# Two transformer blocks on one core: attention heads taken in pairs, the first weight tile loaded in halves, and five reorderings of small vector work

## Chip, cores and metric

One Trainium2 chip, of which the kernel uses one core. The metric is the device time of one execution in microseconds (us); several executions give a median. The engines are TensorE (PE, matrix products and transposes by the identity), VectorE (DVE), ScalarE (ACT), GpSimd (POOL) and SyncE (SP, which here only issues the loads of weights).

## The reference, cut to what matters

Two blocks run one after the other on x of 256 rows by 1024 columns, float32.

```python
for i in range(2):                        # first block
    h = h + (neighbourhood_attention, short_conv_mixer)[i](rms_norm(h))
    h = h + peer_mixer(rms_norm(h))       # top 16 of 2 x 128 keys, 8 heads, 16384 experts
h = rms_norm(h)
# second block
mem_n = rms_norm(mem)
# even layer: heads of 64: 8 over selected blocks (nsa_s), 8 over a window (nsa_w), 8 moba, 4 over mem (mem_e)
#   plus 8 heads over 15 compressed blocks; y = cat(a_out * silu(nz), b_out * silu(mz), m_out * silu(ez)) @ w_out
# odd layer: 4 retention heads, 4 heads over mem (mem_o)
out = rms_norm(odd_layer(even_layer(h)))
```

peer_mixer scores each row against 128 + 128 keys for each of 8 heads, takes the top 16 of each side, the top 16 of their sums, and a weighted sum of `gelu(x @ w_up[e])  * w_down[e]` over the chosen experts. The kernel computes it densely: products with all 16384 rows of w_up, a weight for each (zero where not chosen), and a product with all of w_down.

## The kernel before, in words

All products are done at full float32 precision by splitting each operand into a high part (rounded) and a low part (the rest): high x high, low x high and high x low. A **unit** is a tile of 512 KB of weights, 128 partitions by 1024 numbers, and there are some 730 of them in one fixed order, loaded by SP into a ring of buffers `raw`. ACT copies each into `wh` (line 1458, `highs(end)`: all units up to `end` and a fixed number ahead), DVE subtracts to make `wl` (line 1895, `lows(end)`), and PE multiplies by both. PE takes a unit's high part first, calls `middle`, then takes the low part, then calls `after`. In the order written out by hand, each engine's program says between which units it does its other work.

**Start.** x comes in four parts of 256 KB (`load_x`), the first two of them ahead of the first unit. DVE scales x by the gains, ACT rounds it (`attn_high`), DVE makes the low part (`attn_low`). ACT squares x for the row scales, POOL makes the scales from them, and PE turns them (`turn_rows`).

**Turnovers.** When wo, conv_out, even_out or odd_out ends, DVE adds the product to the residual by quarters (`add_quarters`, line 2012 for wo; line 2010 for conv_out), PE transposes the new residual (`turn`, line 914), DVE scales it (line 1933), ACT rounds it and DVE makes its low part (line 1941), and then the next product starts. wo is taken in the order `WO_ORDER`, which finishes columns 0 to 511 two units ahead of the rest; conv_out takes all four units of one half and then all four of the other.

**peer_mixer.** The query product is followed by the scores; then PE takes the up phase, in which a unit lasts one **tile** of about 2.8 us. Meanwhile DVE finds the top 16 and makes the choices (`pstep`, lines 2143 to 2231). Between its steps it does the low parts: `between(ns)` adds the priced time of a step to a counter and makes a low when the counter has reached `LOW_EVERY`. The prices are written by hand. During the down phase (gated tiles, line 1107) ACT makes `gh` (line 1659) and DVE `gl` (line 2277) for each tile of about 2.7 us. In the second down phase the norm of `mem` is done too: four squares at tile 80 (`norm`), the scales and, at tile 98, `norm_parts` and `norm_split` for all four groups at once.

**Even layer.** 36 units of even_in. PLAN tables say after which unit which step comes: rotation of projections (`rope`, lines 2516 to 2520), transposes, the compressed branch (`vc`, `hid`, `kvc`, `cmp_S`, ...), and from unit 15 on the 28 **heads**. Each head has three steps: S (scores by PE, line 1023; DVE scales and masks them, line 2024, and takes the maximum, line 2038; ACT takes exponents, line 1532), T (PE transposes the weights, line 1028; ACT copies them out of the bank, line 1445) and O (product with v, line 1035; DVE multiplies by the reciprocal of the sum, lines 2654 to 2670). T comes one unit after S and O two units after. There are eight banks in PSUM; four (`other`) go round for all these steps in the order of the jobs, so that a job waits until the job four before it has been read out.

```python
EV_S = (15, 16, 17, 18, 19, 20, 20, 21, 21, 22, 22, 23, 23, 24, 24, 25,
        25, 26, 26, 27, 27, 28, 29, 29, 30, 30, 31, 31)
EV = [(kind, a) for n in range(37) for kind, lag in (("S", 0), ("T", 1), ("O", 2)) ...]
```

## Time and profile before

| what | value |
|---|---|
| median of 3 runs | 2330.66 us (2330.3 to 2331.43) |
| the profiled execution: its own time | 2331.18 us |
| the profiled execution: span in the trace | 2329.4 us |
| mean granted clock of TensorE | 0.999 |
| PE busy | 2302.6 us, 99% of the span |
| DVE, ACT, POOL busy | 1693.9, 1389.1, 128.7 us |
| loaded from memory | 394.5 MB, 170 GB/s over the span |

The profile shows one execution. Busy time is that of an engine's own instructions. A row of a wait names the instruction that waited and the one that released it; L12 is line 12 of the kernel. Names in rows: `bank` is a PSUM bank, `wh`, `wl` the high and low parts of a unit, `x_both` both parts of the normalized input, `arena` and `aux` the working memory, `small` a tile of scalars per row.

### The profile page before, as it was taken

To read this page: it belongs to the slowest core of one execution; us is meant where nothing else is said; L and a number is where in the kernel's file an instruction comes from. 1 tells how busy PE (TensorE), PEld (TensorE's weight loads), DVE (VectorE), ACT (ScalarE), POOL (GpSimd) and SP (SyncE) were. 2 spreads that over 40 slices of the span, in tenths; PEclk is the share of its full clock that TensorE was granted. 3 is DMA by queue.
4 is the path that set the end of the run, shared out by engine and by line. 5 is a ranking of instruction groups with operands and counts; after the bars stand their busy time and mean duration, and the time that the engine had idled before them with its cause. 6 is when DMAs were issued, how large, how long until landed. Compare 5 with 4: busy or idle time off the path is not lost.

```text
span 2329.4 us, 43671 instructions
## 1 busy us (share of the span) xinstructions
PE 2302.6 (99%) x14764; PEld 2032.4 (87%) x14764; DVE 1693.9 (73%) x3202; ACT 1389.1 (60%) x2562; POOL 128.7 (6%) x196
## 2 busy tenths in 40 slices
PE   9999999999999999999999999999999999999998
PEld 8889989999888888999899999988888887788877
DVE  6767996899755555775998799956656668867565
ACT  5646666887545455445666787755554555765554
POOL 1001121000000000000211100000000000000000
PEclk9999999999999999999999999999999999999999
DMA  7455555444566666556555544466665654246454
GB/s 241 134 170 160 186 182 181 144 140 143 177 194 191 194 191 194 177 180 191 172 181 182 167 142 144 148 205 191 193 205 177 197 175 127 82 131 196 136 160 146
DMA packets 137460, 397.58 MB, mean 171 GB/s; under 512 B 12465, under 2 KB 13793, under 8 KB 136545
## 3 DMA queue, kind: packets, MB, share of 16 engines
q1 hardware_dynamic: 134432, 384.71, 53.4%
q0 software_dynamic: 2448, 10.56, 1.3%
q8 instruction: 90, 1.47, 0.3%
q14 instruction: 58, 0.47, 0.1%
q10 hardware_dynamic: 432, 0.36, 0.0%
HBM read 394.54 MB, written 1.05 MB: 170 GB/s over the span
## 4 chain that ended last, share of the span: by engine, by line
PE 86%; DVE 9%; issue 3%; ACT 2%; DVEq 0%; POOL 0%; ACTq 0%; POOLq 0%
PE bank L1107 29%; PE bank L1091 16%; PE bank L976 11%; PE bank L1079 8%; PE bank L982 7%; PE bank L1083 4%; PE bank L1120 4%; DVE wl L1895 2%; PE bank L1035 1%; ACT wh L1458 1%; PE bank L1183 1%; PE bank L1023 1%; PE bank L1028 1%; PE bank L1008 1%; PE bank L1059 1%
## 5 line engine op out<-in xcount | busy, mean ns | idle before, releaser
L1895 DVE TENSOR_TENSOR wl<-raw,wh 128x1024 fp32r<-128x1024 f32 x726 | 886.2, 1222 | 499.9 <-ACT wh L1458 488.1
L1458 ACT ACTIVATE wh<-raw 128x1024 fp32r<-128x1024 f32 x726 | 765.0, 1054 | 616.2 <-PE bank L1107 326.5
L1091 PE MATMUL bank<-x_both,wh 128*128 128x256 f32 x2304 | 303.9, 285 | 0.0
L1091 PEld LDWEIGHTS bank<-x_both,wh 128*128 128x128 f32 x2304 | 285.8, 191 | 0.0
L1107 PE MATMUL bank<-wh,gl 128*128 128x512 f32 x992 | 265.8, 390 | 1.7 <-DVE gl L2277 1.7
L1107 PE MATMUL bank<-wh,gh 128*128 128x512 f32 x992 | 265.5, 389 | 0.5 <-ACT gh L1659 0.5
L1107 PE MATMUL bank<-wl,gh 128*128 128x512 f32 x992 | 265.2, 389 | 0.0
L1079 PE MATMUL bank<-x_both,wh 128*128 128x512 f32 x896 | 224.9, 393 | 0.0
L1107 PEld LDWEIGHTS bank<-wh,gl 128*128 128x128 f32 x992 | 185.8, 188 | 41.9 <-DVE gl L2277 3.5
L1107 PEld LDWEIGHTS bank<-wh,gh 128*128 128x128 f32 x992 | 185.9, 188 | 39.5 <-ACT gh L1659 1.1
L1107 PEld LDWEIGHTS bank<-wl,gh 128*128 128x128 f32 x992 | 186.2, 188 | 38.7
L976 PE MATMUL bank<-wh,x_both 128*128 128x512 f32 (+1 forms) x768 | 195.9, 397 | 1.0 <-ACT wh L1458 0.8
L1079 PEld LDWEIGHTS bank<-x_both,wh 128*128 128x128 f32 x896 | 161.1, 189 | 28.8
L976 PEld LDWEIGHTS bank<-wh,x_both 128*128 128x128 f32 x768 | 139.5, 189 | 31.3 <-issue 4.6
L1091 PE MATMUL bank<-x_both,wl 128*128 128x256 f32 x1152 | 162.9, 284 | 2.3 <-DVE wl L1895 2.3
L1640 ACT ACTIVATE first<-onehot,weight_high 128x128 bf16<-128x128 bf16 x512 | 160.7, 396 | 2.1 <-PE bank L1120 1.8
L1091 PEld LDWEIGHTS bank<-x_both,wl 128*128 128x128 f32 x1152 | 148.3, 192 | 4.5 <-DVE wl L1895 3.9
L1083 PEld LDWEIGHTS bank<-x_both,wl 128*128 128x128 f32 x896 | 122.1, 190 | 9.3 <-DVE wl L1895 0.7
L1575 ACT ACTIVATE halves<-bank 128x512 f32<-128x512 f32 x112 | 67.0, 598 | 101.0 <-PE bank L1083 101.0
L1083 PE MATMUL bank<-x_both,wl 128*128 128x256 f32 x896 | 125.1, 282 | 0.0
L2252 DVE TENSOR_TENSOR first<-onehot,rest_pairs 128x512 bf16<-128x512 bf16 x256 | 99.4, 429 | 26.4 <-PE bank L1120 22.7
L822 POOL TENSOR_TENSOR arena<-halves 128x256 f32 (+1 forms) x112 | 85.7, 765 | 360.1 <-ACT halves L1575 360.1
(327 smaller groups left out, 2883.6 us busy)
## 6 DMA issues: line engine op xcount, KB each, us to landing
raw<-in_w_upT SPq DMA_DIRECT2D x256, 512.0 KB, 3.5
raw<-in_w_down SPq DMA_DIRECT2D x256, 512.0 KB, 4.2
raw<-in_l_w_in SPq DMA_DIRECT2D x84, 512.0 KB, 3.7
raw<-in_peer_w_query SPq DMA_DIRECT2D x32, 512.0 KB, 3.8
raw<-in_l_w_out SPq DMA_DIRECT2D x28, 512.0 KB, 3.3
raw<-in_attn_w_qkv SPq DMA_DIRECT2D x24, 512.0 KB, 4.2
raw<-in_conv_w_in SPq DMA_DIRECT2D x24, 512.0 KB, 3.9
arena<-in_na_bias POOLq DMA_DIRECT2D x4, 1024.0 KB, 6.4
```

The costliest lines, as they stand in the source:

```text
L822: pool.tensor_tensor(acts[:, bass.ds(i * 4 + t, 1), :].rearrange("p a b -> p (a b)"), halves[:, 0], halves[:, 1], ALU.add)\
L976: last = pe.matmul(bank(js[b])[:, 0:cols], lhsT=x[:, kt, b * P:(b + 1) * P], rhs=w[part][:, kk, :], **flags)
L982: last = pe.matmul(bank(js[b])[:, m * SEQ:(m + 1) * SEQ], lhsT=w[part][:, kk, c0:c0 + P], rhs=x[:, kt, :], **f)
L1079: pe.matmul(banks[b].rearrange("p (a b) -> p a b", a=2), lhsT=w[0][:, k, :], rhs=x_both[:, :, k, :], start=k == 0, stop=False, skip_group_ ...
L1083: last = pe.matmul(banks[b][:, 0:SEQ], lhsT=w[1][:, k, :], rhs=xh[:, k, :], start=False, stop=k == KT - 1, skip_group_check=True)
L1091: last = pe.matmul(banks[b][:, 0:SEQ], lhsT=w[part][:, k, :], rhs=x_in[xp][:, k, :], start=(k == 0 and part == 0 and xp == 0), stop=(k == ...
L1107: last = pe.matmul(banks[4 + 2 * m + h][:, :], lhsT=g[gp][:, m * P:(m + 1) * P], rhs=w[:, h * 512:(h + 1) * 512], start=start and part == ...
L1120: last = pe.matmul(banks[2 + q % OUTS][:, c * N_KEYS:(c + 1) * N_KEYS], lhsT=onehot[:, q % RING, c, 1, :], rhs=first[:, q % FIRSTS, p, c, ...
L1458: act.activation(unit_parts(n)[0][:, 0:kts * cols], raw[:, n % RAW, 0:kts * cols], ACT.Copy)\
L1640: ins = act.activation(first[:, q % FIRSTS, 0, c, :], onehot[:, q % RING, c, 0, :], ACT.Copy, scale=weight_high[:, c0:c0 + 1])
L1895: tt(lo[:, 0:kts * cols], raw[:, n % RAW, 0:kts * cols], hi[:, 0:kts * cols].bitcast(F32), ALU.subtract)\
L2252: last = tt(first[:, q % FIRSTS, 1 + p].rearrange("p c (n b) -> p c n b", b=2), onehot[:, s, :, 0].rearrange("p c (n b) -> p c n b", b=2), ...
```

## The change

1. **Start.** The first unit is loaded in two halves of 256 KB with a semaphore each, and ACT rounds it by halves, between its work on x; ACT's squares of parts 0 and 1 of x come first of all; DVE makes the low part of unit 2 ahead of x's parts 2 and 3; there is one more warm-up product.
2. **Turnovers.** In wo and conv_out, DVE makes one low part, not two, ahead of the first two quarters' adds. conv_out is taken in `WO_ORDER`, and the turn comes after its seventh unit (`CONV_TURN`).
3. **Queries.** ACT takes one more unit's high part ahead of its rounding of the last two groups of the rescaled input.
4. **Choices.** `LOW_EVERY` 1400 in place of 1250; new prices; the product with `key_of` in two halves of four heads; the sums and choices of the second stage one or two tiles later.
5. **Memory norm.** One square per tile (80 to 83), scales six tiles later, and the eight rounding steps spread over tiles 98 to 105 by `MEM_STEPS`.
6. **Even and odd layer.** Heads in pairs: the S of a pair at the end of unit n (`EV_AT`), its T between the high and the low part of unit n + 2, its O in the same place of unit n + 3, with one bank for both O. DVE takes one maximum over both heads for each t, one reciprocal, one gate product, and one product for the four outputs of a pair (two where it adds or multiplies into what is there). Three memsets of DVE go to POOL, ahead of the layer; the four copies of `kvc` into the block diagonal become one product with a mask.

```diff
...
-WO_TURN, OUT_TURN, EVEN_TURN, ROWS_AFTER, ROWS_EARLY, ROWS_CONV = 30, 1, 2, 7, 2, 3
+WO_TURN, CONV_TURN, EVEN_TURN, ROWS_AFTER, ROWS_EARLY, ROWS_CONV = 30, 6, 2, 7, 2, 3
...
-EXP_TILES, SUM_TILES, CHOICE_TILES = (26, 54), (30, 59), (34, 62)
+EXP_TILES, SUM_TILES, CHOICE_TILES = (26, 54), (31, 61), (35, 63)
...
-LOW_EVERY = 1250
+MEM_STEPS = ([("whole", 0)], [("whole", 1), ("high", 0)], [("whole", 2), ("high", 1)], [("low", 0), ("high", 2)],
+             [("whole", 3)], [("low", 1), ("high", 3)], [("low", 2)], [("low", 3)])
+LOW_EVERY = 1400
...
-WARM = (7, 5)
+WARM = (7, 6)
...
-EV_S = (15, 16, 17, 18, 19, 20, 20, 21, 21, 22, 22, 23, 23, 24, 24, 25,
-        25, 26, 26, 27, 27, 28, 29, 29, 30, 30, 31, 31)
-EV = [(kind, a) for n in range(37) for kind, lag in (("S", 0), ("T", 1), ("O", 2)) for a in range(len(EV_S)) if EV_S[a] + lag == n]
...
+EV_AT = (16, 18, 20, 21, 22, 23, 24, 25, 26, 27, 28, 29, 30, 31)
+EV_T, EV_O = 2, 3
...
+                        J.add("evO", len(even_pairs(4 * c + u, EV_O)), ring="other")
+                        J.add("evT", 2 * len(even_pairs(4 * c + u, EV_T)), ring="other")
...
+                            J.add("evS", 2, ring="other")
...
+            for kk, done in enumerate((first_landed, landed[0])):
+                sp.dma_start(raw[:, 0, kk * CHUNK:(kk + 1) * CHUNK], units[0][0][:, kk, :]).then_inc(done, 16)
...
+            pool.memset(cmp_small[:], 0.0)
+            pool.memset(cmp_s, 0.0)
+            pool.memset(block_mask, 0.0).then_inc(mask_cleared, 1)
+            pool.wait_ge(mask_cleared, 1)
+            for i in range(4):
...
+            def pair_outputs(name, p):
+
+                j = take(name + "O", p)
+                for i in range(2):
+                    wait_read(pe, turned_at(name, p, i))
+                    family, _, qT, kT, v = pair_heads[name][2 * p + i]
+                    for t in range(TT):
+                        n = key_tiles(family, t)
+                        for kt in range(n):
+                            last = pe.matmul(bank(j)[:, (i * TT + t) * HEAD:(i * TT + t + 1) * HEAD],
+                                             lhsT=turned_of(name, head_base[name] + 2 * p + i)[:, weight_tiles(family).index((kt, t)), :],
+                                             rhs=v[kt], start=(kt == 0), stop=(kt == n - 1))
+                done(last, j)
...
+            def even_middle(n):
...
-            for c in range(2):
-                project("conv_out", "N", conv_out, k=2 * c, ready=lambda k0: split_ready("conv", k0 // 2 + 1),
-                        after=lambda u: c == 1 and u == OUT_TURN and turn("peer1", "conv", (0, 1)))
+            project_in("conv_out", conv_out, WO_ORDER, lambda i: i == CONV_TURN and turn("peer1", "conv", (0, 1)),
+                       lambda k0: split_ready("conv", k0 // 2 + 1))
...
-            def norm(src, ready, then=None):
-
-                for p in range(4):
-                    ready(p + 1)
-                    c, t = p // 2, p % 2
-                    act.activation(squares[:, p], src[:, t, c * 512:(c + 1) * 512], ACT.Square,
-                                   accum_out=small[:, 2 * t + c:2 * t + c + 1]).then_inc(squared, 1)
-                if then:
...
-                        highs(query + ROWS_AFTER + 2)
-                        highs(query + ROWS_AFTER + 3)
+                        for ahead in (2, 3, 4):
+                            highs(query + ROWS_AFTER + ahead)
                         norm_split(f"rescaled{layer}", some=(2, 3))
...
-                    norm(view(0, TT, D), lambda p: act.wait_ge(extra_loaded["mem"], 16 * TT))
-                    gated_tiles(MEM_SQUARES, MEM_SPLIT)
-                    norm_split("mem", mem_in_T)
-                    gated_tiles(MEM_SPLIT, TAIL[0] - SPLIT)
+                    for p in range(4):
+                        gated_tiles(MEM_SQUARES + p, MEM_SQUARES + p + 1)
+                        mem_squared(p)
+                    gated_tiles(MEM_SQUARES + 4, MEM_SPLIT)
+                    for k, steps in enumerate(MEM_STEPS):
+                        gated_tiles(MEM_SPLIT + k, MEM_SPLIT + k + 1)
...
+            for p in range(2):
+                squared_part(None, p)
             attn_high(0, 0, first_whole, first_high)
+            first_weights_high(0, first_weights)
+            attn_high(1, 0, first_whole, first_high)
+            first_weights_high(1, hi_ready)
+            issued[0] = 1
             attn_high(0, 2, x_whole, x_high)
-            attn_high(1, 0, first_whole, first_high)
-            highs(first_unit["qkv"] - 1)
             attn_high(1, 2, x_whole, x_high)
+            for p in range(2, 4):
+                squared_part(None, p)
...
             norm_split("attn", some=(2, 3))
...
+                        for p in even_pairs(4 * c + u, EV_T):
+                            pair_turned("ev", p)
                         highs(first_unit["even_in"] + KT // UKT * c + u + 1)
                         if u == KT // UKT - 1:
...
-                lows(start, 2)
+                lows(start, 1 if out_name in ("wo", "conv_out") else 2)
                 add_quarters(out_name, (0, 1))
                 lows(turn, 2)
...
-                        pstep(tt(by_head, by_head, key_of[:, :, i].unsqueeze(2).to_broadcast([P, PEER_HEADS, TOPK, TOPK]), ALU.mult), 1200)
-                        for w, ns in ((8, 700), (4, 430), (2, 300)):
+                        for h0 in range(0, PEER_HEADS, PEER_HEADS // 2):
+                            some = by_head[:, h0:h0 + PEER_HEADS // 2]
+                            pstep(tt(some, some, key_of[:, h0:h0 + PEER_HEADS // 2, i].unsqueeze(2)
+                                     .to_broadcast([P, PEER_HEADS // 2, TOPK, TOPK]), ALU.mult), 730)
+                        for w, ns in ((8, 730), (4, 460), (2, 450)):
                             pstep(tt(pick[:, :, 0:w], pick[:, :, 0:w], pick[:, :, w:2 * w], ALU.add), ns)
-                        pstep(tt(top_out(t, i), pick[:, :, 0], pick[:, :, 1], ALU.add))
+                        pstep(tt(top_out(t, i), pick[:, :, 0], pick[:, :, 1], ALU.add), 430)
...
-                    gated_tiles(TRIG + 25, MEM_SQUARES)
+                    gated_tiles(TRIG + 25, MEM_SQUARES + 6)
                     norm_scale("mem")
-                    gated_tiles(MEM_SQUARES, MEM_SPLIT)
...
+                    for k, steps in enumerate(MEM_STEPS):
+                        gated_tiles(MEM_SPLIT + k, MEM_SPLIT + k + 1)
+                        for kind, g in steps:
+                            if kind == "whole":
+                                whole("mem", g)
+                            elif kind == "low":
+                                lower("mem", g, mem_in_T)
...
+            lows(first_unit["qkv"], 2)
             for g in range(2, 4):
                 whole("attn", g)
-            lows(first_unit["qkv"], 2)
...
-                        dve.memset(cmp_small[:], 0.0)
...
-                        for i in range(4):
-                            ins = dve.tensor_copy(vbd[32 * i:32 * i + 32, k, i, :], bank(j)[32 * i:32 * i + 32, 64:64 + HEAD])
-                        read_out(ins, j)
+                        read_out(tt(vbd[:, k], bank(j)[:, 64:64 + HEAD].unsqueeze(1).to_broadcast([P, 4, HEAD]),
+                                    block_mask.unsqueeze(2).to_broadcast([P, 4, HEAD]), ALU.mult), j)
...
-                            step(dve.memset(cmp_s, 0.0))
...
+                top = pair_of(pair_top, p)
+                if family in CAUSAL:
+                    for t in range(TT):
+                        ins = dve.tensor_reduce(top[:, :, t], slots[:, :, t, 0:key_tiles(family, t) * P], AX, ALU.max, negate=True)
+                else:
+                    ins = dve.tensor_reduce(top, slots, AX, ALU.max, negate=True)
+                ins.then_inc(scores_shifted, 2)
...
+                step(dve.reciprocal(pair_scale, pair_sums[:, n % 8:n % 8 + 2]))
...
+                read_out(tt(pair_tmp, out_, by_row, ALU.mult), j)
+                step(tt(dst, dst, pair_tmp, op))
...
-                    even_heads(even_heads_at(4 * c + u, "S"))
+                    for p in even_pairs(4 * c + u, EV_O):
+                        pair_outputs("ev", p)
+                    for p in even_pairs(4 * c + u):
+                        pair_scores("ev", p)
                     if c < len(EVEN_COLS):
                         lows(first_unit["even_in"] + KT // UKT * c + u + 1)
...
```

## Rows read from the trace of the kernel before

**Rows 1.** The page, part 1: busy time and share of the span by engine.
```profile
PE 2302.6 (99%) x14764; PEld 2032.4 (87%) x14764; DVE 1693.9 (73%) x3202; ACT 1389.1 (60%) x2562; POOL 128.7 (6%) x196
```
**Rows 2.** Waits of PE: line <- who released it: total us, times, longest.
```profile
PE bank L982 <- ACT wh L1458: 2.3, 4, 0.9
PE bank L1091 <- DVE wl L1895: 2.3, 4, 0.6
...
PE bank L1107 <- DVE gl L2277: 1.7, 2, 1.4
...
PE bank L914 <- DVE resid L2012: 1.0, 2, 0.7
```
**Rows 3.** Timeline of PE, start: start, length, work [idle before <-releaser].
```profile
8.65 2.15 PE L982 MATMUL bank<-x_both,wh 128*128 128x256 f32 x16 [0.88 <-ACT wh L1458]
...
15.43 1.22 PE L982 MATMUL bank<-x_both,wl 128*128 128x256 f32 x8 [0.87 <-DVE wl L1895]
```
**Rows 4.** DMA issues, first 30 us: count, KB each, median us to landing.
```profile
raw<-in_attn_w_qkv SPq DMA_DIRECT2D x11, 512.0 KB, 4.8
...
resid<-in_x SPq DMA_DIRECT2D x4, 256.0 KB, 4.7
```
**Rows 5.** Timeline of PE and of DVE at the turn in wo.
```profile
138.09 0.71 PE L982 MATMUL bank<-x_raw_h,wh 128*128 128x256 f32 x4 [0.26 <-DVE x_raw_l L1941]
```
```profile
132.72 0.68 DVE L2012 TENSOR_TENSOR resid<-bank,resid 128x512 f32<-128x512 f32 x1
```
**Rows 6.** Timeline of PE in conv_out.
```profile
1031.82 0.70 PE L976 MATMUL bank<-wh,conv_out_h 128*128 128x512 f32 x2 [0.41 <-DVE conv_out_l L2475]
```
**Rows 7.** Timeline of PE in the query product of layer 0.
```profile
175.15 0.71 PE L982 MATMUL bank<-x_raw_h,wh 128*128 128x256 f32 x4 [0.59 <-ACT wh L1458]
```
**Rows 8.** Timeline of DVE in the choices of layer 0.
```profile
265.65 0.88 DVE L2230 TENSOR_TENSOR pick<-pick 128x512 bf16<-128x512 bf16 x2
266.56 0.40 DVE L2231 TENSOR_TENSOR arena<-pick 128x128 f32<-128x128 bf16 x1
266.99 1.23 DVE L2225 TENSOR_TENSOR pick<-places,lanes 128x2048 bf16<-128x2048 bf16 x1
268.25 1.23 DVE L1895 TENSOR_TENSOR wl<-raw,wh 128x1024 fp32r<-128x1024 f32 x1
```
**Rows 9.** Timeline of PE at the second half of the memory norm.
```profile
1789.90 1.20 PE L1107 MATMUL bank<-wh,gh 128*128 128x512 f32 x4 [0.49 <-ACT gh L1659]
```
**Rows 10.** Windows: length, then busy us (instructions) of PE, PEld, DVE, ACT, POOL, granted clock, DMA share, GB/s.
```profile
1905.00:2068.00 163.00, 156.28 (x954) 125.98 (x953) 131.50 (x347) 101.78 (x212) 0.00 (x0) 0.99 0.36 105
```
```profile
1959.00:1963.00 4.00, 4.00 (x17) 3.28 (x15) 3.60 (x9) 1.57 (x5) 0.00 (x0) 0.57 0.46 131
```
**Rows 11.** Timeline of PE among the even layer's heads.
```profile
1958.61 0.52 PE L1028 MATMUL bank<-ident,aux 128*128 128x128 f32 x3 [1.52 <-ACT aux L1532]
1958.89 3.36 PE L976 MATMUL bank<-wh,x_both 128*128 128x512 f32 x8
```
```profile
1976.08 2.11 PE L976 MATMUL bank<-wh,x_both 128*128 128x512 f32 x8
```
**Rows 12.** Groups of DVE, 1905 to 2068 us: count, busy us, mean ns, idle before.
```profile
L2024 DVE SCALAR_TENSOR_TENSOR aux<-bank,aux 128x256 f32<-128x256 f32 x24 | 9.9, 413 | 0.0
L2038 DVE TENSOR_REDUCE small<-aux 128x1 f32<-128x256 f32 x24 | 9.8, 408 | 0.0
...
L2517 DVE TENSOR_TENSOR arena<-arena,aux 128x512 f32<-128x512 f32 x6 | 4.2, 692 | 0.2
...
L2662 DVE TENSOR_SCALAR arena<-bank,small 128x64 f32<-128x64 f32 x16 | 3.8, 280 | 0.3
```
**Rows 13.** Timeline of ACT at the third family's exponents and its silu.
```profile
2051.18 0.51 ACT L1532 ACTIVATE aux<-aux,small 128x256 f32<-128x256 f32 x1
...
2051.80 1.28 ACT L1732 ACT_TABLE_LOAD   x1
2053.09 1.58 ACT L1732 ACTIVATE arena<-arena 128x512 f32<-128x512 f32 x2
```

More of the change, by code:

```diff
@@ L401, in build @@
         weight("conv_in", d["conv_w_in"], 3 * D, CONV_CHUNKS)
-        weight("conv_out", d["conv_w_out"], D)
+        weight_in("conv_out", d["conv_w_out"], WO_ORDER)
         weight("query1", d["peer_w_query"][1], 2048)
@@ L1542, in attention, with pair_exponents, pair_turned @@
                         evac(turned_of(name, n).rearrange("p a b -> p (a b)")[:, 0:w], j, bank(j)[:, 0:w])
+            def pair_exponents(name, p):
+                for i in range(2):
+                    n, family = head_base[name] + 2 * p + i, pair_heads[name][2 * p][0]
+                    act.wait_ge(scores_shifted, n + 1)
+                    for t in range(TT):
+                        row = scores_of(name, n)[:, t, 0:key_tiles(family, t) * P]
+                        ins = act.activation(row, row, ACT.Exp, bias=pair_top[:, n % 4, t:t + 1],
+                                             accum_out=sums_of(name, n)[:, t:t + 1])
+                    ins.then_inc(weights_ready, 1)
+            def pair_turned(name, p):
+                for i in range(2):
+                    w = len(weight_tiles(pair_heads[name][2 * p][0])) * P
+                    j = turned_at(name, p, i)
+                    evac(turned_of(name, head_base[name] + 2 * p + i).rearrange("p a b -> p (a b)")[:, 0:w], j, bank(j)[:, 0:w])
             def peer(layer):
@@ L2295, in gated_tiles @@
                 def gated_tiles(t0, t1):
-                    with dve.Fori(0, (t1 - t0) // 4) as i:
-                        for k in range(t0, t0 + 4):
-                            low(d0 + k, i)
-                            gated_low(k, i)
+                    if t1 - t0 >= 4:
+                        with dve.Fori(0, (t1 - t0) // 4) as i:
+                            for k in range(t0, t0 + 4):
+                                low(d0 + k, i)
+                                gated_low(k, i)
                     for t in range(t1 - (t1 - t0) % 4, t1):
@@ L2476, in _ @@
                             conv_out[0][:, 2 * g:2 * g + 2].bitcast(F32), ALU.subtract), x_low, n)
[L2477 to L2478 removed]
+            start = first_unit["conv_out"] + CONV_TURN
+            turnover("peer1", "conv_out", start, start, first_unit["query1"], x_raw)
             peer(1)
```

239 lines of the change are left out of this document (129 added, 110 removed).

## The prediction

> **What bounds the kernel now.** I read the busy times first. PE is busy for 2302.6 of the 2329.4 us of the span [rows 1], and the change leaves the number of its products alone, but for one more warm-up. So it can win only what PE waits, about 27 us with both ends of the kernel, plus time in which PE is slow. DVE is at 73% and ACT at 60% [rows 1]; their work costs nothing unless PE stands for it. Then I read the waits of PE by releaser [rows 2], and the timeline of PE around each place that the diff touches [rows 3, 6, 7, 9, 11]. The reader is to see many short stalls, none over 1.6 us. They cost more than the bracket shows: successive groups overlap (a group that starts at 1958.61 and lasts 0.52 ends after the next one's start, 1958.89 [rows 11]), and a stall breaks the overlap. So I add 0.15 us to each bracket.
>
> **Start.** PE's first true product waits 0.88 us for ACT's cast of unit 0, the low part of unit 1 waits 0.87 for DVE [rows 3]. With halves, ACT casts 512 columns at a time, and PE begins some 0.5 us earlier, but the low of unit 0 still comes behind both casts. DVE's earlier order takes off most of the second wait, and the squares ahead of ACT's other work take off a later one of some 0.5 us for the row scales. Against it: a 256 KB load took a median 4.7 us to land where 512 KB took 4.8 [rows 4], so a half load is hardly sooner by itself. Value -1.0; bounds 0 (the second half lands as the whole did, and the low part sets the pace) and -1.8 (both waits go).
>
> The Trainium skill (DMA: Bandwidth & Descriptors, Bandwidth) has a rule that speaks against it: batch transfers to 1 MiB or more. Here it agrees with rows 4 in that halves gain little; by it the load's part would be nought and the term about -0.6.
>
> **Turn in wo.** The first add's wait and the second's sum to 1.0 us [rows 2]. The adds take 0.68 [rows 5] and stand behind a low of 1.23 [rows 8] that the change puts after them: both waits go, about 1.3 with restarts. That low and what follows are then later by 1.2 less the stall saved: the wait of the query's first product, 0.26 [rows 5], grows by 0.4 or so. Value -0.8; bounds -0.3 and -1.3.
>
> **Conv_out.** It waits 0.41 us for the low part of the convolution's rows [rows 6], which goes on, since the cast of the next unit is behind ACT's casts of the rows too. In WO_ORDER one unit is left to cover the turn's second half instead of two, a unit being 2.7 us here, while DVE must do two adds of about 0.7 [rows 5], two scalings and two low parts (0.69 each), some 4.1 us. I take +0.8; bounds -0.3 and +1.5.
>
> **Queries.** 0.59 us at 175.15 [rows 7], and its like in layer 1: ACT's cast stands behind its rounding. One cast more ahead takes both off: -1.5 with restarts; bounds -0.8 and -1.5 (its rounding of groups 2 and 3 comes one cast later, which has slack).
>
> **Choices.** Four waits of up to 0.6, 2.3 together [rows 2], and some 0.1 to 0.2 us each for restarts, and again at a second place just behind each: 4.5 in all. The cause is the price list: 0.88 + 0.40 + 1.23 us of steps stand between two lows (265.65 to 268.25) [rows 8], since 430 + 300 + 300 stays below 1250 and the next step is started. With the new prices (460 + 450 + 430, then 1250) that does not fit: no stretch between lows has more than about 1.6 us of steps. A tile is about 2.8 us, a low is 1.23, so 1.6 just fits. Value -3.9; bounds -3.3 and -4.5.
>
> **Memory norm.** DVE's four wholes and lowers stand ahead of a `gl`: 1.7 us in two waits [rows 2], 0.49 for ACT's `gh` [rows 9]; with restarts, and ACT's squares before the first, 3.1. Spread, each tile gets at most two of these steps (0.7 to 0.9 each). In a tile of 2.7 us DVE has 1.23 of low and 0.42 of `gl`, ACT 1.06 and 0.40: 1.0 and 1.2 are left, and the queues have some slack from tile to tile. Value -2.9; bounds -2.3 and -3.1.
>
> **Even layer.** In 1905 to 2068 PE is idle for 163.0 - 156.3 = 6.7 us [rows 10]; with 15 restarts 9.0. On top, after the 1.52 us wait at 1956.7 the granted clock of 1959 to 1963 is 0.57 [rows 10], so mostly the lower of its two levels (1.2 and 2.4 GHz), and eight products take 3.36 us for the usual 2.11 [rows 11]; with six smaller ones, 1.6 lost. So 10.6 is there to win, this with the compressed part's 2.0 at 1914 to 1931.
> What DVE gets back, per pair of masked heads: one reduce of 0.41 for t = 1 becomes one of 0.69 for two (0.82 before), likewise for t = 0, so 0.3; the outputs, four of 0.28 [rows 12], become one of about 0.43, so 0.7; one reciprocal and one gate product go, 0.3. That is 1.3 of about 4.6 us, over 14 pairs about 15 us (less for those that add), and 1.4 of memsets and 0.5 of copies: 17 of DVE's 131.5 us [rows 10]. But the total of DVE is not what makes PE wait; what does is order. I wrote down for each unit when PE, DVE and ACT could start each step, with the durations of such rows; three places come out late:
> (a) T of the first pairs comes one and a half units (about 6 us with the heads' own products) after S. The chain is 0.62 + 0.83 for masking and 0.4 + 0.7 for the maxima on DVE, a cast of 1.06 ahead on ACT, and four exponents of 0.4 to 0.51 with 0.12 after each (2.3): 5.9. It is met or missed by up to 1 us: 1.9 over two pairs.
> (b) Around units 19 to 22 DVE has two rotations, each four steps of 0.4 to 0.69 [rows 12] for two t, 4.5 us, beside lows and pairs of 3.3. It falls some 3.9 behind a unit of 4.6. At the end of unit 22 the transposes of `even_T` 8 need the bank that held the first T of pair 2, and ACT frees it only after the exponents of pair 3, which wait for DVE: 3.0 us, and 1.0 before it.
> (c) The T of the first `mem` pair: ACT has exponents of 2.0 and more, then a table load of 1.28 and silu of 1.58 [rows 13], then a cast, and only then the turned copies that the O in the middle of unit 33 waits for: 1.5.
> The compressed part keeps 1.6 of its 2.0. The memsets stand on POOL ahead of the load of the compression weights, and delay it by some 2 us; POOL does nothing at all from 1905 on [rows 10], and the load is issued long before, so I put that at 0 (if the cover were gone, 2). That makes 9.0 for 9.0 of before, and the clock: the 3.0 wait is twice the one that took it down before. I give that 6 in 10: 0.9 for 1.6. Value -0.7. Bounds: nothing of (a) to (c) comes, -8; or all come in full, and 3.2 of the slow clock, +2.
>
> The Trainium skill (TensorE: Matmul & The Clock Gate, Part 1: The HAM clock gate) says that the array's clock falls by half when idle and comes back after sustained activity. The 0.57 in rows 10 agrees. [...]
>
> **Odd layer.** No wait of PE at its four heads before; the pairs keep its lags of a unit or more: 0, and with its cover gone no more than the 0.5 of one such wait.
>
> **Sum.** -1.0 - 0.8 + 0.8 - 1.5 - 3.9 - 2.9 - 0.7 = -10.0. The profiled execution took 2331.2, so 2321.2 for it; the median is 0.5 lower, so 2320.7. I say 2321.
>
> **Rivals.**
> *New waits in the even layer (0.20).* (b) and (c) come in full, the clock falls twice, and conv_out loses 1.5. For it: four banks for more jobs in a bunch, DVE's 81% of 163 us. Against: five bank jobs per pair where there were six. -10.0 + 2.7 + 0.7 = -6.6; with turnovers at their poor bounds -5: 2325.
> *All goes through (0.18).* DVE's 17 us come out of the stalls directly, (a) to (c) stay below 0.5 each: even layer -7, conv_out 0, the rest as in the sum: -17: 2314. For it: before, the waits of this stretch fall where DVE is busy nearly throughout. Against: (b) is one bunch of work that the pairs do not thin out.
> *The choices gain nothing (0.09).* The real step times drift off the new prices, or the lows are late elsewhere: the sum without -3.9 is -6: 2324.5.
> *Slower (0.05).* DVE falls behind in the up phase. Up to 1.4 of priced steps and then one of up to 1.25 can come between two lows: 1.25 + 1.4 + 1.23 = 3.9 us against a tile of 2.8. It decides if the mean of steps between lows is above 2.8 - 1.23 = 1.6 us. Then each tile costs the excess; 0.2 us over 56 tiles in two layers is +22: 2343. Against: the top-16 steps, 0.28 each, are stopped finely, at 1.4 to 1.6; the mean stays at 1.43 by the old trace's counts.
> My forecast has 0.48.
>
> **Range and chances.** 2316 to 2326: the forecast's own range is 2318 to 2324; the first and third rival lie inside, of the second 0.15 of its 0.18 is below, and the slower one's 0.05 above, which leaves out 0.2. A difference of under 0.2%, 4.7 us, is about what a measurement of this kernel can't tell from none: faster is below 2326.0. From the cases: the forecast 0.47 faster, the first rival 0.14 of its 0.20, all goes through 0.18, the third 0.07 of its 0.09: 0.86. Same: 0.09. Slower: 0.05.
>
> **What would show it.** PE's waits at L914 for DVE's adds at 133 and at L982 for ACT at 174 and 1085 gone; no wait at L1091 for wl over 0.2; no bracket on L1107 near 1736 and 1789; near unit 22 of even_in one wait of 2 to 3 us at the transposes, released by ACT's copy, followed by a clock of about 0.6. I am wrong if the up phase's tiles lengthen (DVE), or if the even layer shows waits under 0.5 only (then it is 2314), or if in conv_out a wait above 1.5 us comes up.

## The result, and the profile after

The changed kernel takes 2315.4 us (median of 4 runs, 2314.09 to 2316.47) against 2330.74 (4 runs, 2330.3 to 2331.43): 0.9933 of before, 95% interval 0.9921 to 0.9946. It is faster by 15.3 us. The forecast was 2321, in 2316 to 2326, so the result lies just below the range. It is beside the rival "all goes through" (2314), though not for that rival's reason. The profiled execution took 2316.47, with a span of 2314.7: 14.7 less than before's.

From page part 1 of the changed kernel, as in [rows 1]:

```profile
PE 2293.9 (99%) x14765; PEld 2029.5 (88%) x14765; DVE 1678.2 (73%) x3109; ACT 1382.6 (60%) x2563; POOL 130.2 (6%) x203
```

PE's busy time is 8.7 us less, with the same products and one more. Part of that belongs to stalls, since the ends of products are modelled and one that stands before a stall counts longer; part, as the next section shows, is PE's own work getting shorter, which the prediction did not look for.

The waits of PE, as in [rows 2]:

```profile
PE bank L1259 <- ACT aux L1500: 2.3, 1, 2.3
PE bank L998 <- DVE x_raw_l L2027: 1.7, 4, 0.5
PE bank L1087 <- ACT aux L1500: 1.5, 1, 1.5
PE bank L1395 <- DVE warm L2449: 1.5, 1, 1.5
PE bank L998 <- DVE x_both L2465: 1.4, 1, 1.4
PE bank L1063 <- ACT arena L1500: 1.2, 1, 1.2
```

(A row is: the product that waited and its line, who released it, total us, times, longest. L998 and L1143 do now what L982 and L1091 did before.) All four groups of [rows 2] are gone. The new ones at L1259, L1087 and L1063 are the even layer's. Of L998's two rows, the four waits on `x_raw_l` are the first products of the two queries, behind the turns, and the one on `x_both` is the first true product.

Since PE issues the same sequence of products apart from the places changed, one and the same product can be looked up in both traces. Its start shows how much had been gained by then:

| the same product, start in us | before | after | gained so far | of this part | predicted |
|---|---|---|---|---|---|
| qkv, early | 30.01 | 28.42 | 1.59 | start 1.59 | 1.0 |
| query of layer 0 | 150.06 | 147.22 | 2.84 | turn in wo 1.25 | 0.8 |
| query's end | 186.02 | 182.36 | 3.66 | cast ahead 0.82 | 0.75 |
| up phase, past the choices | 360.08 | 354.59 | 5.49 | choices 1.83 | 1.95 |
| conv_in | 1010.07 | 1004.52 | 5.55 | 0.06 | 0 |
| query of layer 1 | 1060.07 | 1055.07 | 5.00 | conv_out -0.55 | -0.8 |
| scores of layer 1 | 1100.07 | 1094.25 | 5.82 | cast ahead 0.82 | 0.75 |
| up phase, past the choices | 1280.00 | 1272.42 | 7.58 | choices 1.76 | 1.95 |
| down phase, past the norm | 1800.16 | 1789.39 | 10.77 | memory norm 3.19 | 2.9 |
| even_in, early | 1905.17 | 1894.40 | 10.77 | 0 | 0 |
| turn after even_out's start | 2068.10 | 2053.29 | 14.81 | even layer 4.04 | 0.7 |
| odd_out | 2300.21 | 2285.49 | 14.72 | odd layer -0.09 | 0 |

Six of the seven terms (the two casts and the two layers' choices counted together) came within 0.6 us. The even layer's came 3.3 us larger. Windows of that stretch, as in [rows 10] (the first is the whole of it, 1905 to 2068 before):

```profile
1894.40:2053.30 158.90, 152.12 (x954) 124.21 (x953) 116.91 (x254) 96.16 (x212) 0.00 (x0) 0.99 0.37 109
1974.00:1978.00 4.00, 4.00 (x18) 3.28 (x16) 1.77 (x4) 2.97 (x10) 0.00 (x0) 0.62 0.51 150
```

PE is idle for 158.90 - 152.12 = 6.78 us; it was 6.72 [rows 10]. DVE does 14.6 us less and PE waits as long as before. The clock fell once here too, to 0.62 for 4 us. So neither waits nor clock gave the 4.04: it is the 4.16 us by which PE's busy time is shorter, over as many products (954).

The timeline of PE shows the two places (b) and (c) where the prediction had put its new waits, and the slow products behind (b):

```profile
1970.02 0.93 PE L1063 MATMUL bank<-arena 64*128 64x128 f32 x8
1973.27 0.76 PE L1259 MATMUL bank<-ident,arena 128*128 128x128 f32 x4 [2.32 <-ACT aux L1500]
1973.68 3.64 PE L992 MATMUL bank<-wh,x_both 128*128 128x512 f32 x8
...
2038.55 1.97 PE L1087 MATMUL bank<-arena,aux 128*128 128x64 f32 x16 [1.47 <-ACT aux L1500]
```

Which of PE's own work got shorter is seen from windows of a single line. First the scores (S), then T, then O, each over the whole stretch; columns: length, PE busy, PEld busy, clock, DMA share, GB/s. Changed kernel:

```profile
1894.40:2053.30 158.90, 14.09 (x112) 8.28 (x112) 0.99 0.37 109
1894.40:2053.30 158.90, 12.24 (x88) 10.04 (x88) 0.99 0.37 109
1894.40:2053.30 158.90, 21.26 (x176) 21.87 (x176) 0.99 0.37 109
```

The kernel before, same lines of source:

```profile
1905.00:2068.00 163.00, 17.03 (x112) 9.93 (x112) 0.99 0.36 105
1905.00:2068.00 163.00, 13.85 (x88) 9.32 (x88) 0.99 0.36 105
1905.00:2068.00 163.00, 21.96 (x176) 22.71 (x176) 0.99 0.36 105
```

The same 112 products of S take 2.9 us less. These busy times overlap with those of the products beside them, so they don't add up. Taken from the start of each product to the start of the next, with the waits left out, the whole stretch is 4.1 us shorter, and that adds up: S 15.68 before and 13.18 after, T 10.65 and 8.82, O 18.71 and 18.89, all else 111.2 and 111.2. So 2.5 us are the scores' and 1.8 the transposes'. The timeline of PE before says how. Once a single head was scored, once two:

```profile
1964.08 0.92 PE L1023 MATMUL bank<-arena 64*128 64x128 f32 x4
1964.93 0.55 PE L1028 MATMUL bank<-ident,aux 128*128 128x128 f32 x3
...
1974.92 0.93 PE L1023 MATMUL bank<-arena 64*128 64x128 f32 x8
```

Four products take 0.92 us and eight take 0.93. A score contracts over 64 numbers, so it uses 64 rows of the array, and head 2p lies on partitions 0 to 63, head 2p + 1 on 64 to 127. When the two follow each other the second costs nothing. Before, six visits of PE in this stretch scored one head alone; after the change there is none, so there are three visits fewer, of 0.85 us each to the start of the next product.

The Trainium skill states it (TensorEngine Tiling (Array Packing), Tiling Modes, Key Properties): tiles of the array work independently, and a change of tiling mode drains the array. The 0.93 for eight agrees with the first. By the starts in the trace, the step from a head's last score product to the product of 128 rows behind it takes 0.31 us, where the one before it, of the same length and followed by another of 64 rows, takes 0.22, which agrees with the second; fewer visits pay it fewer times.

T has the other part. A first transpose behind a score steps 0.16 us to the next one, behind a product of O 0.12; with some 15 of them, that is 0.7 of the 1.8. The rest lies in fewer visits and in fewer transposes that stand before a stall and count 0.27 us for the usual 0.11. This is read from the starts; no run moved T alone.

### The profile page after: what moved, and what is told of

Its sections match the earlier page's. It is cut to its first block, busy times and chain, and to the rows that moved or that the text cites. A ratio compares the mean times of both kernels' runs of the same rounds, so it can differ in the third digit from the quotient of the medians.

```text
span 2314.7 us, 43481 instructions
## 1 busy us (share of the span) xinstructions
PE 2293.9 (99%) x14765; PEld 2029.5 (88%) x14765; DVE 1678.2 (73%) x3109; ACT 1382.6 (60%) x2563; POOL 130.2 (6%) x203
## 3 DMA queue, kind: packets, MB, share of 16 engines
q8 instruction: 90, 1.47, 0.3%
## 4 chain that ended last, share of the span: by engine, by line
PE 91%; DVE 5%; ACT 2%; issue 2%; DMA 0%; SPq 0%; DVEq 0%; POOLq 0%; POOL 0%; ACTq 0%
PE bank L1159 29%; PE bank L1143 18%; PE bank L992 11%; PE bank L1131 9%; PE bank L998 8%; PE bank L1135 5%; PE bank L1172 4%; PE bank L1024 1%; DVE wl L1981 1%; PE bank L1235 1%; PE bank L1087 1%; PE bank L1111 1%; PE bank L1051 1%; PE bank L1003 0%; ACT wh L1513 0%
## 5 line engine op out<-in xcount | busy, mean ns | idle before, releaser
L1981 DVE TENSOR_TENSOR wl<-raw,wh 128x1024 fp32r<-128x1024 f32 x726 | 886.5, 1222 | 497.9 <-ACT wh L1513 485.0
L1143 PE MATMUL bank<-x_both,wh 128*128 128x256 f32 x2304 | 304.2, 285 | 0.1
L1143 PEld LDWEIGHTS bank<-x_both,wh 128*128 128x128 f32 x2304 | 285.7, 191 | 0.9 <-ACT arena L1638 0.9
L1143 PE MATMUL bank<-x_both,wl 128*128 128x256 f32 x1152 | 161.9, 283 | 0.0
L1143 PEld LDWEIGHTS bank<-x_both,wl 128*128 128x128 f32 x1152 | 148.5, 192 | 0.4
```

The source lines that it names most:

```text
L1143: last = pe.matmul(banks[b][:, 0:SEQ], lhsT=w[part][:, k, :], rhs=x_in[xp][:, k, :], start=(k == 0 and part == 0 and xp == 0), stop=(k == ...
L1981: tt(lo[:, 0:kts * cols], raw[:, n % RAW, 0:kts * cols], hi[:, 0:kts * cols].bitcast(F32), ALU.subtract)\
```

## Experiments

Effects of a few us are compared by the span of the profiled run and by the starts of the same product, against those of the changed kernel. Of these runs, seven have the changed kernel's start as it is. In them the product at 28.42 starts between 0.20 us earlier and 0.50 later; from there to the even layer the difference drifts by at most 0.2 where nothing was changed. So each run brings an offset of its own from the start, and one run can't show an effect of under some 0.5 us there. A gain or loss is against the changed kernel's 2314.7, where nothing else is said.

### The even layer's part alone

The kernel before with part 6 of the change and nothing else: the diff is the part of it shown above that has `EV_AT`, `pair_...`, the memsets and the block mask.

> The kernel before with part 6 of the change alone (heads in pairs in both layers, memsets on GpSimd, the product with the block mask). Nothing of the computation is left out. If the gain of the even layer is its own and comes from TensorE's own time, the span is 2329.4 - 4.0 = 2325.4 (2324.9 to 2325.9), with the gain between unit 15 of even_in and even_out and nowhere else, the idle time of that stretch near the 6.7 us of before and its busy time 4 us less. If the gain needs the other parts (the load order, another state of the queues), it comes out by more than 1 us elsewhere.

2326.94 us (10 runs, 2325.28 to 2328.11) against 2330.47 (13 runs): 0.9983, interval 0.9974 to 0.9993. The span is 2325.3 for the 2325.4 expected. Ahead of the even layer a product starts 0.11 us earlier than before; at the turn the gain is 4.09, at the end 4.03. Window of the stretch:

```profile
1905.00:2064.00 159.00, 152.26 (x953) 124.20 (x953) 116.94 (x254) 96.37 (x212) 0.00 (x0) 0.99 0.37 109
```

Idle 6.74, busy 4.0 less: the gain is this part's own, and it is busy time. (The clock fell once here too.)

### Nothing but the heads' schedule

```diff
-EV_S = (15, 16, 17, 18, 19, 20, 20, 21, 21, 22, 22, 23, 23, 24, 24, 25,
-        25, 26, 26, 27, 27, 28, 29, 29, 30, 30, 31, 31)
+EV_S = (16, 16, 18, 18, 20, 20, 21, 21, 22, 22, 23, 23, 24, 24, 25, 25,
+        26, 26, 27, 27, 28, 28, 29, 29, 30, 30, 31, 31)
```

> The kernel before with nothing but the table of units of the heads changed: heads 2p and 2p+1 are scored after the same unit for all 14 pairs (16, 18, 20, 21 ... 31), where before seven pairs or so had their two heads one unit apart. T stays one unit later and O two. Theory A (two scores of 64 rows that follow each other run at once in the two halves of the array, so a second head in the same visit is free): TensorE's busy time at the score products falls from 17.0 to about 14.1 us, as in the changed kernel, and the busy time of 1905 to 2068 by 2.5 to 3.5. Theory B (the gain comes from VectorE's shorter work): the score products stay near 17.0, since VectorE's work is as before. The waits may grow in either case, with T only one unit behind.

One table of numbers, with DVE's and ACT's work instruction by instruction as before. Windows of 1905 to 2066.8: S alone, then all engines.

```profile
1905.00:2066.80 161.80, 14.77 (x112) 8.91 (x112) 0.99 0.36 106
...
1905.00:2066.80 161.80, 154.51 (x955) 125.13 (x954) 131.71 (x347) 102.04 (x212) 0.00 (x0) 0.99 0.36 106
```

S falls from 17.03 to 14.77: most of the 2.9, with VectorE's busy time at 131.7 (131.5 before). (It was to be 14.1; in two pairs here the second head's bank came free late and they took 1.48 us, see the last section.) Theory B is out. The whole stretch is only 1.8 us shorter in busy time, below the 2.5 to 3.5 expected, and the gain at its end is 1.2. T, still one unit behind S, now waits 4.5 us for ACT where it waited 1.8, though all idle time together is 7.29 us for 6.72. T keeps 13.88 us here, against 12.24 in the changed kernel. So the rest of the gain goes with T's new place, one unit later and directly behind O instead of S. No run has T there with VectorE's work as before, so whether VectorE's 15 us less was needed to hold the waits at 6.8 is not shown.

### A product between the two heads

```diff
+                    if i == 1:
+                        pe.transpose(bank(j)[:, 0:P], ident[:], ident[:])
```

> The changed kernel with one transpose of the identity (128 rows, 128 columns) put on TensorE between the two heads of each pair of scores, into the bank that the second head then overwrites, 14 in the even layer and 2 in the odd one. Theory A (the two heads overlap only when one follows the other directly): the pair takes 0.85 + 0.3 + 0.85 in place of 0.86 us, so about +1.15 each, +14 to +18 in all less what the waits of the stretch (9 us) absorb: span +8 to +17. Theory B (no overlap of products, the pair is short for another reason): each transpose costs what it takes itself, 0.11 to 0.3: +2 to +5.

Span 2326.1, +11.4, inside theory A's range. Timeline of PE at one pair:

```profile
1966.28 0.92 PE L1065 MATMUL bank<-arena 64*128 64x128 f32 x4
1967.13 0.33 PE L1062 MATMUL bank<-ident 128*128 128x128 f32 x1
1967.40 0.92 PE L1065 MATMUL bank<-arena 64*128 64x128 f32 x4
```

From the first start the next group of PE starts 1.96 us later; in the changed kernel it is 0.86 (1965.54 to 1966.40). All 12 pairs of this kind now take 1.96 us, and the four longer ones (the last two and the odd layer's) 2.37 for 1.07, so a pair adds 1.10 or 1.30 where no wait absorbs it. The small product costs 0.26; the other 0.84 is the overlap lost. Window of the stretch:

```profile
1894.70:2062.10 167.40, 165.46 (x968) 131.95 (x967) 117.97 (x254) 97.04 (x212) 0.00 (x0) 1.00 0.36 102
```

PE is busy for 13.3 us more, its idle time falls from 6.78 to 1.94, and the clock doesn't fall at all, which gives back some 1.6. This settles how S got shorter; T's share it leaves open.

### The waits of the even layer

```diff
...
-                            pair_turned("ev", p)
+                            if p != 2:
+                                pair_turned("ev", p)
...
+                        if 4 * c + u == 21:
+                            pair_turned("ev", 2)
...
-    ... (7, 3): [("silu", 2), ("silu", 0)],
-    (8, 0): [("nsa_y", 0)], ...
+    ... (7, 3): [("silu", 2)],
+    (8, 0): [("silu", 0)], (8, 1): [("nsa_y", 0)], ...
```

> The changed kernel with two changes of order on ScalarE in the even layer: the turned weights of pair 2 are copied out of their banks ahead of the exponents of pair 3, and the second silu comes one unit later (its reader on VectorE too). Theory: the wait of 2.3 us at 1973 is ScalarE's copy behind the exponents, and the clock of 0.62 just behind it follows from that wait: both go, -2.6 and -1.6, and the wait of 1.47 at 2038.5 shrinks by about 1: -5.2 in all, span 2309.5. Rival 1: VectorE's lateness is the cause, so the wait comes back one or two steps later at a bank or a turned weight: -1 to -3. Rival 2: the clock falls anyway, as the waits of 1.2 and less add up: -3.6.

Span 2310.7: -4.0. By the product starts 3.05 comes by 1975, 0.32 by 1980 and 0.92 by 2043, 4.3 in all; the start was 0.28 later by chance. The place of (b), same columns as above:

```profile
1970.28 0.93 PE L1063 MATMUL bank<-arena 64*128 64x128 f32 x8
1971.14 0.66 PE L1259 MATMUL bank<-ident,arena 128*128 128x128 f32 x4
1971.56 2.08 PE L992 MATMUL bank<-wh,x_both 128*128 128x512 f32 x8
...
1977.01 0.93 PE L1063 MATMUL bank<-arena 64*128 64x128 f32 x8 [0.52 <-ACT arena L1500]
```

The 2.32 us wait is gone, and the eight products take 2.08 for 3.64. A wait of 0.52 has come up behind it, and PE's gain at this place is 3.05 + 0.32 where 2.6 + 1.6 was expected. That lies between the theory and rival 1: ScalarE's order was the wait, and VectorE's lateness is the next one: before ScalarE's copy that released the 0.52, its exponents at 1974.61 had stood 0.56 for VectorE's maximum. Rival 2 is out in this run, where the clock never fell in the even layer; but whether it falls varies from run to run (last section), so the 1.6 of the clock is not shown to be the edit's.

### Unit 0 in one load

> The changed kernel with unit 0 loaded in one piece of 512 KB; ScalarE still casts it by halves, in the same order. Theory A (the half is worth something: in the changed kernel ScalarE's first cast starts at 6.61, released by the load, and the first product at 8.12): the first cast starts at about 7.1 to 7.2 and the first product 0.3 to 0.6 later; by unit 2 it is still 0.2 to 0.6 late. Theory B (halves gain nothing, the gain of the start is all from the order of ScalarE's and VectorE's work): within 0.1.

```diff
-            for kk, done in enumerate((first_landed, landed[0])):
-                sp.dma_start(raw[:, 0, kk * CHUNK:(kk + 1) * CHUNK], units[0][0][:, kk, :]).then_inc(done, 16)
+            load(0)
...
-                act.wait_ge((first_landed, landed[0])[kk], 16)
+                act.wait_ge(landed[0], 16)
```

The first cast starts at 6.89 for 6.61, and the first product at 8.40 for 8.12, at the lower end of theory A. That 0.3 is real: in the eight traces of kernels with the two halves the first product starts at 8.03 to 8.15. By unit 2 it can't be told from chance: the product at 28.42 is 0.25 us late here, and in the seven other runs with the halves it is anywhere from 0.20 early to 0.50 late. So the halves bring the first product forward by 0.3 of its 0.5 us (8.65 before), and how much of the start's 1.6 is theirs stays open. The span is 2316.8, 2.1 above the changed kernel. Some 0.4 of it is there ahead of the even layer, and the other 1.65 came in one place that the edit doesn't touch, behind the 1.5 us wait of (c). Windows of this run there:

```profile
2034.50:2038.50 4.00, 3.01 (x15) 2.17 (x13) 0.56 (x3) 3.97 (x8) 0.00 (x0) 1.00 0.37 131
2038.50:2042.50 4.00, 3.52 (x21) 3.55 (x22) 1.84 (x2) 1.99 (x3) 0.00 (x0) 0.67 0.00 0
```

and of the changed kernel, where the same wait left the clock alone:

```profile
2038.50:2042.50 4.00, 3.95 (x30) 3.76 (x31) 2.27 (x2) 2.85 (x5) 0.00 (x0) 1.00 0.00 0
```

### The prices of the choices

```diff
-                                 lane.to_broadcast([P, HK, TOPK // 2, 2]), ALU.is_equal), 1250)
+                                 lane.to_broadcast([P, HK, TOPK // 2, 2]), ALU.is_equal), 1200)
...
-                                     .to_broadcast([P, PEER_HEADS // 2, TOPK, TOPK]), ALU.mult), 730)
-                        for w, ns in ((8, 730), (4, 460), (2, 450)):
+                                     .to_broadcast([P, PEER_HEADS // 2, TOPK, TOPK]), ALU.mult), 600)
+                        for w, ns in ((8, 700), (4, 430), (2, 300)):
...
-                        pstep(tt(top_out(t, i), pick[:, :, 0], pick[:, :, 1], ALU.add), 430)
+                        pstep(tt(top_out(t, i), pick[:, :, 0], pick[:, :, 1], ALU.add))
```

> The changed kernel with the prices of the choices' steps as before (the two halves of the product at 600 each), LOW_EVERY at 1400 still. Theory (prices below the real times let 2.5 us of steps stand between two low parts): waits of 0.3 to 0.7 come back in each of the four places, +2 to +4 us in all, span 2317 to 2319. Rival (the two halves of the product alone made the difference): within 1 us of the changed kernel.

Span 2321.7, +7.0, above the 2 to 4 expected: 1.2, 2.2, 1.1 and 2.1 us at the four places (263 to 269, 339 to 349, 1171 to 1178, 1248 to 1258), 0.2 at the start and nothing after them. The wait PE L1143 <- DVE wl L1981 is 4.6 us in ten pieces, of 0.7 at most; before the change it was 2.3 in four [rows 2]. So the price list decides, as the theory says, and the rival is out. With LOW_EVERY at 1400 the old prices are worse than they were with 1250, since the choices of the kernel before took 3.6 us more than the changed kernel's, and these take 6.7 more.

### A larger LOW_EVERY

> The changed kernel with LOW_EVERY at 1650 in place of 1400. Theory: a tile of the up phase lasts 2.8 us and a low part 1.23, so VectorE keeps up while the mean of its steps between two low parts is below 1.6 us. At 1650 the mean is some 1.75: each of about 56 tiles of each layer lasts 0.1 to 0.2 longer, +8 to +22 us. Rival (there is slack of some other kind, as low parts run ahead): under +3.

```diff
-LOW_EVERY = 1400
+LOW_EVERY = 1650
```

Span 2347.0, +32.4, all of it in the two up phases (16.3 and 16.0). Timeline of PE in the choices of layer 0:

```profile
248.27 1.21 PE L1135 MATMUL bank<-x_both,wl 128*128 128x256 f32 x8 [1.12 <-DVE wl L1981]
249.32 2.00 PE L1131 MATMUL bank<-x_both,wh 128*128 128x512 f32 x8
252.54 1.22 PE L1135 MATMUL bank<-x_both,wl 128*128 128x256 f32 x8 [1.22 <-DVE wl L1981]
```

The rival that was to be slower exists, at a step 250 ns further: tiles of 4.2 us (248.27 to 252.54), and no slack. It costs more than the estimate, since in the choices the steps are coarse: there four stretches in a row, from the end of one low to the start of the next, last 2.95, 2.63, 2.51 and 2.09 us (244 to 259), and over the whole up phase the mean is 1.83.

### A version better than both

> The changed kernel with the two reorderings of the run on the even layer's waits, with conv_out in the order of before (and its two low parts ahead of the adds), and with ScalarE's evacuations at unit 19 of even_in turned round: the bank of the compressed weights and of even_T 7 ahead of the two of the chunk. By the sum: 2314.7 - 4.0 - 0.55 - 1.2 = 2308.9 of span, median about 2310; ratio to before 0.991. If the wait at 1958 only moves on (the chunk's evacuation is late for the rotations that VectorE does next), 2310.2.

```diff
...
+                        if 4 * c + u == 19:
+                            even_steps(c, u)
...
```

This puts ScalarE's copies of `cmp_T` and `even_T` 7 ahead of the chunk; the edits of the run on the waits and conv_out as before go with it. 2313.74 us (5 runs, 2312.92 to 2314.82), 0.9929 of before (0.9916 to 0.9943). Span 2311.2, neither 2308.9 nor 2310.2. conv_out gives its 0.56 and the wait at 1958 its 1.45, but then the transposes of pair 2 wait:

```profile
1966.40 0.50 PE L1074 MATMUL bank<-ident,aux 128*128 128x128 f32 x3
1969.38 0.55 PE L1074 MATMUL bank<-ident,aux 128*128 128x128 f32 x3 [2.48 <-DVE arena L2768]
```

for the bank with the outputs of pair 1, which VectorE reads only after the rotation; the rotation had itself waited for the chunk. VectorE is the bound at units 19 to 21, and what PE gains ahead of it is lost there.

> The kernel of the run before (e8) without its reordering at unit 19: so the changed kernel with the two reorderings on ScalarE in the even layer (pair 2's turned weights, the second silu) and conv_out as before. Theory: in e8 the chunk's evacuation came later, so VectorE's rotation too, and the transposes of pair 2 waited 2.5 us for the bank that VectorE read last. Without it span 2314.7 - 4.0 - 0.55 = 2310.1, 1.1 below e8. Rival: the 2.5 us wait of e8 comes from pair 2's copies being early; then it is here too and the span is 2311 or more.

```diff
-                        if 4 * c + u == 19:
-                            even_steps(c, u)
```

2311.79 us (5 runs, 2311.12 to 2312.71), 0.992 of before (0.9906 to 0.9933), span 2310.0 for the 2310.1 expected. This is the best kernel here: its median is 3.6 us below the changed kernel's. The two were not measured side by side and their intervals against before overlap, but their runs don't (2311.12 to 2312.71, 2314.09 to 2316.47). In the traces 4.7 us of span lie between them, some 1.6 of it the clock, which falls in the changed kernel's and not in e9's. The 2.5 us wait is gone, so it did not come from pair 2's early copies alone.

> As e9, and the second rotation of the last projection (rope 11) one unit later, with the transposes of even_T 8 and 9 one unit later too. Theory: VectorE's lateness at units 20 to 22 is what is left of the waits there (0.5 to 1.4 us at 1958 and 1976); with a unit between the two rotations it is made up in part: the wait at 1976 goes, -0.7, span 2309.4. Rival: VectorE has no slack in these units, so the wait only moves on: within 0.3 of e9.

```diff
...
-    ... ("rope", 10)], (5, 0): [("rope", 11)],
+    ... ("rope", 10)], (5, 1): [("rope", 11)],
...
-    (5, 2): [("even_T", 8)], (5, 3): [("even_T", 9)], ...
+    (5, 3): [("even_T", 8)], (6, 0): [("even_T", 9)], ...
```

2312.23 us (5 runs, 2311.67 to 2314.33), span of the profiled run 2312.5; its fastest runs (2311.67, 2311.68) are within 0.6 of e9's fastest. The theory is out; the rival holds in kind, at a little more than its 0.3. Of the 2.5 us between the two spans 0.5 is there at the start, by chance. The edit itself costs some 0.5: e9's wait of 0.47 at 1976 is gone, but the pair behind it takes 1.94 us to the next product for 0.86, its second head late for its bank:

```profile
1977.46 0.92 PE L1063 MATMUL bank<-arena 64*128 64x128 f32 x4
1978.55 0.92 PE L1063 MATMUL bank<-arena 64*128 64x128 f32 x4 [0.17 <-DVE arena L2765]
```

The other 1.6 is the clock, which fell behind the 1.2 us wait at 1958, as the window of 1961 to 1965 shows; e9 had the same wait and kept its clock:

```profile
1961.00:1965.00 4.00, 4.00 (x14) 3.07 (x12) 3.60 (x9) 2.39 (x7) 0.00 (x0) 0.61 0.29 111
```

## Why the prediction was wrong

**The step that failed** is in its first paragraph: "So it can win only what PE waits, ... plus time in which PE is slow." Because the number of PE's products was the same, their cost was taken as the same. It isn't: what a product of 64 rows costs depends on its neighbour. The even layer's term was then made of waits alone, -0.7. On those it was right: it took 9.0 of waits for 9.0 of before, and the idle time is 6.78 for 6.72; it named both new places, (b) at 3.0 us (2.32 and its restart) and (c) at 1.5 (1.47); it gave the fall of the clock 6 in 10, and it fell. With waits as before and the clock falling once as before, its own account comes to 0.0, and 4.04 was measured. What it left out is 4.1 us of PE's own time: 2.5 at S and 1.8 at T, from start to start, with O and the rest unchanged. The run of the schedule alone and the run of the split pairs show the share of S. The share of T, which stands a unit later and behind O now, was only read from traces.

The second rival's time (2314) is nearly the measured one by a mechanism that did not act: it had VectorE's 17 us come out of the stalls, and with 14.6 us less of VectorE's work PE stood as long as before.

**Start.** 1.6 for 1.0, inside its bounds, with a scatter of the start of 0.7 between runs. The first product came 0.5 us earlier, as said, 0.3 of it by the half load. How the rest divides between load and order is not shown.

**Turn in wo.** 1.25 for 0.8. Both waits at L914 went; the two later waits became 0.38 and 0.39 (at 135.20 and 142.44) from 0.26 and 0.35, a growth of 0.1 where 0.4 was taken.

**Conv_out.** 0.55 lost for 0.8. Undone in e8 and e9 (the first two kernels of the last experiment), it came back (0.56, 0.54). The wait of 0.42 for the convolution's low part stayed, as said; the new ones are 0.38 and 0.52 at the query.

**Queries, choices, memory norm.** 1.64 for 1.5, 3.6 for 3.9, 3.2 for 2.9. The first and the last lie 0.1 outside their own bounds. In each the named waits are gone, and the run with the old prices confirms the cause given for the choices. The sentence that no stretch between lows keeps more than about 1.6 us of steps does not hold: ahead of the choices (255.21 to 257.67) one of 2.4 us stays, in both halves of both layers, and no wait of PE is listed for it. One such stretch is covered; several in a row, as with LOW_EVERY at 1650, are not. And what stands between lows is not 460 + 450 + 430 of prices, which would stay below 1400, but 730 + 460 + 450 and then 430 + 1250.

**The slower rival.** It was given 0.05, with 1.6 us of steps between lows as the point where it decides. LOW_EVERY at 1650 is past it and costs 32 us; 1400 isn't.

## What to carry to other kernels

Count what the busiest engine itself pays for an order, not only what it waits: before saying that its work is unchanged, compare the mean of one instruction in different neighbourhoods, as four products in 0.92 us and eight in 0.93. Products that use half of the array's rows should stand in pairs on opposite halves with nothing between them, and the bank of the second must be free when the first starts. And a hand-written interleaving by price is only as good as its prices: a few prices 30 to 150 ns too low cost 7 us against the changed kernel, and 250 ns of threshold 32, where the right ones had gained 3.6.

## What the runs showed of the hardware that was not expected

A pair of heads overlaps only if both banks are free in time, and a pair that has lost its overlap shows as busy time, not as a wait. The only one in the changed kernel took 1.55 us, not 0.93 (timelines of ACT and of PE):

```profile
1959.09 1.23 ACT L1500 ACTIVATE arena<-bank 128x512 f32<-128x512 f32 x2
1959.73 1.55 PE L1063 MATMUL bank<-arena 64*128 64x128 f32 x8 [1.21 <-ACT arena L1500]
```

ACT's first copy ends at 1959.68 and frees the first head's bank, and its four products start at 1959.73; the second copy ends at 1960.31, and the second head's start at 1960.36. The wait before the pair is not the cause: in the run on the waits a pair came behind a wait of 0.52 us and took 0.93, shown above, and in e8 a pair without any wait before it (1957.96) took 1.40, its second head starting at 1958.44 behind ACT's copy that ended at 1958.39. The same explains the two pairs of 1.48 in the run of the schedule alone and the pair in e10.

Whether the clock falls after a wait is not set by the wait's length in these traces. It fell after 2.32 (to 0.62 over 4 us), after 1.47 in one run and after 1.2 in another; it held at 1.00 after 1.47 and 1.2 in others, and after 2.48 in e8. It fell in all five traces that have the 2.3 us wait of (b). Each fall costs some 1.6 us (1.65 and 1.57 by the product starts in the run with one load and in e10). That is as much as most of the spread between the runs of one kernel (2314.09 to 2316.47, 2311.67 to 2314.33), but only one run of each has a trace, so it is not shown to be the cause. A wait of over 1.2 us here costs itself and a chance of 1.6 more.
